# Two-layer hybrid attention and convolution backbone: key, query, value and statistics pieces moved in TensorE's order, and the rms root computed by ScalarE and VectorE

## The chip, the cores and the metric

One of the eight cores of a Trainium2 chip runs the whole program. The metric is the device time of one execution in microseconds (us). TensorE is called PE in the profile, its weight load PEld, VectorE DVE, ScalarE ACT, GpSimd POOL, and SyncE SP. SP issues nearly all DMAs, in order; each engine runs its own instructions in order and waits on semaphores for the others.

## What is computed

Two layers over 1024 latent tokens and 256 context tokens of width 1024. The second layer needs only keys and values of the context tokens. Cut to what matters:

```python
u   = h * (1 + scale) + shift                     # adaLN, per stream
p   = u @ w_in                                     # q k v z_a | s_b s_c s_h z_s | c_a c_g z_c | three gates
q   = rope(rms_norm(q) * q_gain);  k = rope(rms_norm(k) * k_gain)     # 8 query heads, 2 kv heads, 64 wide
o   = softmax(q k^T / 8) v                         # over context + latent keys, 128-query blocks
A   = (o * silu(z_a)) @ w_pa
B   = (s_b * conv3(s_c * s_h) * silu(z_s)) @ w_ps
hc  = conv31(c_a * sigmoid(c_g)) + b
C   = (silu(layer_norm(hc)) * silu(z_c)) @ w_pc + b_pc
h   = layer_norm(alpha * h + gate * ((sig(g_a) A + sig(g_b) B + sig(g_c) C) @ w_out))
# rms_norm(x) = x * rsqrt(mean(x^2) + 1e-6), per head
```

## The kernel before

Everything is held transposed: channels on the 128 partitions, tokens along the row, T = 1280 columns in layer 0 and 1024 in layer 1 (keys and values always 1280). A matrix product is made of fp32r parts, hi and lo: each `job(n)` makes one tile of 128 output channels as w_hi x_hi + w_lo x_hi + w_hi x_lo, over K = 8 blocks k of the contraction (K = 4 for the branch projections), in chunks of 512 columns. A k block so has 9 matmuls in layer 0 (6 of 512 and 3 of 256 columns) and 6 in layer 1. Jobs alternate between two PSUM slots (`SLOT`, n % 2); `sfree` says that a slot was read. The weights of job n come by an SP load (`load`, wraw, two buffers) and are split into wh and wl by GpSimd (`split`, a cast L584 and a subtraction L586 for each half); the load of job n waits for the split of job n-2, and the split waits for the end of job n-2.

A layer goes through these stages.

- **Query, key, value** (jobs 0 to 5: k, q0, q1, q2, q3, v). ScalarE copies each product to fc (`evac`), TensorE turns it into token order in pieces of up to four 128x128 transposes (`turn_piece`, L736), which go through two small PSUM banks in turns (`tbank(f)`, f % 2); `t_free` says that a piece was read. The pieces are put inside later jobs by hooks that run ahead of block k: K in job 1, Q0 in job 2, Q1 in job 3 (k = 2, 3, 5), the six pieces of the finished keys kd in job 4 (`keys_inside`, k = 1 to 6), Q2 and Q3 in job 5. For each of k, q0 to q3 ScalarE copies the pieces to raw (L1047) and squares (`square`), VectorE sums and scales (`mean_square`, L1348 and L1349), GpSimd raises to the power -1/2 (`rms`, L610, once in its queue for each n, behind the splits), and VectorE applies root, gain and rotation (`normed`, L1354 on). `k_hi` copies the turned keys to raw and rounds them to kT; `k_lo` on VectorE takes the remainder. raw has two buffers, and `s_rawfree` counts in the order K, Q0, Q1, KT0, KT1, Q2, Q3, V.
- **Attention** (`att_units`: 16 units of 10 key tiles for the latent queries in each layer, 4 short ones of 2 tiles in layer 0). In step kt of a unit TensorE turns four 128x128 blocks of the probabilities (`turn_probs`, L864) into bank kt % 2, ScalarE copies them (L1138), VectorE takes the remainder (L1454) and frees the bank. At even kt below 8 the scores of one head of the next unit are made (`scores`, L855), VectorE takes their maximum (L1428), and ScalarE the exponentials at the next odd kt (L1118). At kt = 5 the query of the unit after next is turned into bank 0 (`q_fill`, L841), copied by ScalarE (`q_hi`, L1110) and freed by VectorE (`q_lo`, L1420). `pv` (L877) multiplies two steps later. TensorE fills each step with matmuls of the 24 merge-gate jobs (`gate_slice`, L824), whose results ScalarE sends to DRAM.
- **Convolution** (jobs 30 to 61): z_a, conformer and short branch; the 31 taps run on VectorE (L1487).
- **z_c and the conformer norm** (jobs `I_ZC` to `I_ZC`+3). The channel sum and the sum of squares over partitions are matmuls with a matrix of ones (`stat`, L742), sent through the two small banks.
- **Merge** (24 jobs `I_M`+q of K = 4: branch B for q < 8, A for q < 16, C for the rest). SP loads the gate of each q (`load_gate`, waits for the use of gate q-2) and the attention branch (`load_ya`) between the weight loads; ScalarE takes the sigmoids and rounds the attention branch (`attn_hi`, L1230), VectorE multiplies (L1600, L1602), and in between does the conformer norm (L1555, L1574), `conf_out` and `attn_lo` (L1583).
- **Output** (8 jobs), the post norm, and between the layers the second modulation.

## Time and profile before

| | |
|---|---|
| median of three runs | 2879.9 us (2878.3 to 2881.8) |
| the profiled execution, its own time | 2872.59 us |
| its span in the profile | 2870.8 us |
| mean granted TensorE clock | 0.978 |
| busy: PE | 2677.8 us, 93% |
| busy: DVE | 1511.9 us, 53% |
| busy: ACT | 820.9 us, 29% |
| busy: POOL | 907.0 us, 32% |

The sum of busy TensorE time and its pauses is the span. Busy time contains matmuls at half clock, so a pause can cost more than its own length. Idle time of the other three engines costs nothing by itself. Durations in the rows are of one instruction or of a merged run ("x4"); a figure in square brackets is the engine's idle time before it and what ended that.

### The profile page before, as it was taken

What the parts mean: (1) busy time and instruction counts of PE and PEld (TensorE: products, weight loads), DVE (VectorE), ACT (ScalarE), POOL (GpSimd) and SP (SyncE); (2) the same over time, 40 slices, a digit from 0 to 9 for tenths busy, and PEclk for the clock granted to TensorE, in tenths of its full rate; (3) what the DMA queues carried; (4) which work ended last, traced back from release to release, by engine and by line L of the source; (5) the groups of instructions that cost most, each with busy time, mean ns of one, the idle gap of its engine ahead of it and who ended that gap; (6) DMA issues with size and microseconds to landing.
All of it is one profiled execution on the core that took longest, in us unless ns stands there. A gap on an engine that the chain in (4) does not pass through costs nothing.

```text
span 2870.8 us, 32327 instructions
## 1 busy us (share of the span) xinstructions
PE 2677.8 (93%) x13560; PEld 2197.1 (77%) x13560; DVE 1511.9 (53%) x1410; ACT 820.9 (29%) x1156; POOL 907.0 (32%) x819
## 2 busy tenths in 40 slices
PE   7999999999999999999995899999999999999993
PEld 4778888887887888788883677777788888877882
DVE  3454444441019988845626444554540199875635
ACT  3234444442100000142213434444441000014313
POOL 3431111111225333334531342111113355544550
PEclk8999999999999999999998999999999999999996
DMA  6010110011241111133343311101012211123421
GB/s 253 30 61 34 34 37 34 34 43 57 75 163 65 32 43 38 48 118 121 128 162 133 135 48 46 40 34 41 34 41 81 74 52 44 45 70 125 144 95 66
DMA packets 65521, 212.12 MB, mean 74 GB/s; under 512 B 7520, under 2 KB 10848, under 8 KB 63328
## 3 DMA queue, kind: packets, MB, share of 16 engines
q1 hardware_dynamic: 47520, 179.11, 17.8%
q10 hardware_dynamic: 17856, 30.94, 2.9%
q8 instruction: 108, 1.77, 0.3%
q14 instruction: 37, 0.30, 0.0%
HBM read 164.93 MB, written 45.09 MB: 73 GB/s over the span
## 4 chain that ended last, share of the span: by engine, by line
PE 83%; DVE 7%; ACT 6%; issue 2%; DMA 1%; POOL 1%; SPq 0%; ACTq 0%; DVEq 0%; POOLq 0%
PE PS L695 46%; PE PS L824 19%; PE PS L855 5%; PE PS L864 5%; PE PS L877 5%; DVE cv L1487 2%; ACT Pr L1118 2%; ACT PTh L1138 1%; PE PS L887 1%; DVE qTl L1420 1%; DVE e L1555 1%; PE PS L736 1%; PE PS L742 1%; DMA wmA<-wmod 1%; DVE e L1563 1%
## 5 line engine op out<-in xcount | busy, mean ns | idle before, releaser
L584 POOL CAST wh<-wraw 128x512 fp32r<-128x512 f32 (+1 forms) x376 | 297.7, 792 | 1476.5 <-PE PS L695 805.6
L586 POOL TENSOR_TENSOR wl<-wraw,wh 128x512 fp32r<-128x512 f32 (+1 forms) x376 | 534.3, 1421 | 30.1
L1454 DVE TENSOR_TENSOR PTl<-PS,PTh 128x512 fp32r<-128x512 f32 x328 | 226.9, 692 | 423.1 <-ACT PTh L1138 423.1
L1487 DVE SCALAR_TENSOR_TENSOR cv<-hc,vec,cv 128x1024 f32<-128x1024 f32 x360 | 441.7, 1254 | 8.2
L695 PE MATMUL PS<-Uh,wh 128*128 128x512 f32 (+1 forms) x1536 | 428.3, 377 | 17.0 <-ACT Uh L1023 15.7
L695 PE MATMUL PS<-Uh,wl 128*128 128x512 f32 (+1 forms) x1536 | 420.1, 371 | 0.0
L695 PE MATMUL PS<-Ul,wh 128*128 128x512 f32 (+1 forms) x1536 | 418.9, 371 | 0.0
L824 PE MATMUL PS<-Uh,wh 128*128 128x512 f32 (+1 forms) x960 | 358.4, 373 | 1.2 <-ACT stg L1076 1.2
L824 PE MATMUL PS<-Ul,wh 128*128 128x512 f32 (+1 forms) x960 | 359.3, 374 | 0.0
L824 PE MATMUL PS<-Uh,wl 128*128 128x512 f32 (+1 forms) x960 | 359.0, 374 | 0.0
L1138 ACT ACTIVATE PTh<-PS 128x512 fp32r<-128x512 f32 x328 | 196.4, 599 | 480.0 <-PE PS L864 479.0
L695 PEld LDWEIGHTS PS<-Uh,wh 128*128 128x128 f32 x1536 | 266.9, 190 | 70.8 <-issue 17.2
L695 PEld LDWEIGHTS PS<-Uh,wl 128*128 128x128 f32 x1536 | 268.1, 189 | 54.2
L695 PEld LDWEIGHTS PS<-Ul,wh 128*128 128x128 f32 x1536 | 266.6, 188 | 53.6
L864 PE MATMUL PS<-ident,Pr 128*128 128x128 f32 x1312 | 198.8, 274 | 37.6 <-DVE qTl L1420 37.0
L864 PEld LDWEIGHTS PS<-ident,Pr 128*128 128x128 f32 x1312 | 158.9, 141 | 83.1 <-DVE qTl L1420 45.5
L1428 DVE TENSOR_REDUCE nm<-PS 128x1 f32<-128x1280 f32 (+1 forms) x144 | 196.0, 1365 | 40.3 <-PE PS L855 40.1
L824 PEld LDWEIGHTS PS<-Uh,wh 128*128 128x128 f32 x960 | 180.9, 188 | 35.1 <-ACT stg L1076 1.7
L824 PEld LDWEIGHTS PS<-Uh,wl 128*128 128x128 f32 x960 | 180.9, 188 | 33.4
L824 PEld LDWEIGHTS PS<-Ul,wh 128*128 128x128 f32 x960 | 180.7, 188 | 33.2
L1118 ACT ACTIVATE Pr<-PS,nm 128x1280 f32<-128x1280 f32 (+1 forms) x144 | 177.4, 1232 | 29.3 <-DVE nm L1428 29.3
L855 PE MATMUL PS<-kT,qTh 128*128 128x512 f32 (+1 forms) x400 | 152.0, 380 | 12.4 <-ACT Pr L1118 9.4
(153 smaller groups left out, 3275.8 us busy)
## 6 DMA issues: line engine op xcount, KB each, us to landing
wraw<-w SPq DMA_DIRECT2D x140, 512.0 KB, 3.4
graw<-stg ACTq DMA_DIRECT2D x96, 256.0 KB, 2.0
e<-graw SPq DMA_DIRECT2D x24, 640.0 KB, 3.9
wraw<-w SPq DMA_DIRECT2D x48, 256.0 KB, 4.1
wmL<-wmod SPq DMA_DIRECT2D x8, 1536.0 KB, 11.7
e<-graw SPq DMA_DIRECT2D x24, 512.0 KB, 3.6
wmA<-wmod SPq DMA_DIRECT2D x8, 1024.0 KB, 12.9
hL<-hT_in SPq DMA_DIRECT2D x8, 640.0 KB, 21.8
```

Source lines behind the costliest of these rows:

```text
L584: nc.gpsimd.tensor_copy(wh[par][:, s], wraw[par][:, s]).then_inc(whi[par], 1)
L586: nc.gpsimd.tensor_tensor(wl[par][:, s], wraw[par][:, s], wh[par][:, s].bitcast(F32), ALU.subtract).then_inc(wsplit[par], 1)
L695: ins = mmul(PS[:, at + c:at + c + m], w[par][:, k * P:(k + 1) * P], x[:, k, c:c + m], start=(first and a == 0), stop=(last and a == 2))
L824: ins = mmul(PS[:, FB[x % 2]:FB[x % 2] + m], w[n % 2][:, k * P:(k + 1) * P], u[:, k, c:c + m], start=(r == 0), stop=(r == 23))
L855: ins = mmul(PS[:, s0 + c:s0 + c + m], x[un % 2][:, h * P:(h + 1) * P], kT[:, g, k0 * P + c:k0 * P + c + m], start=(a == 0), stop=(a == 1))
L864: ins = nc.tensor.transpose(PS[:, PT0[bank] + h * P:PT0[bank] + (h + 1) * P], Pr[:, un % 2, h, kt * P:(kt + 1) * P], ident[:])
L877: ins = mmul(PS[:, O0:O0 + 512], Vt[:, k0 + kt, g, :], x[b][:], start=(kt == 0 and a == 0), stop=(kt == nk - 1 and a == 1))
L1118: fn(Pr[:, g, h, :nk * P], PS[:, s0:s0 + nk * P], ACT.Exp, bias=nm[:, m:m + 1], accum_out=rs[:, g, h:h + 1]).then_inc(s_exp, 1)
L1138: fn(PTh[(sb + step) % 3][:], PS[:, PT0[bank]:PT0[bank] + 512], ACT.Copy).then_inc(pt_hi[bank], 1)
L1428: nc.vector.reduce_max(nm[:, m:m + 1], PS[:, s0:s0 + nk * P], AX_X, negate=True).then_inc(s_nm, 1)
L1454: tt(PTl[b][:], PS[:, PT0[bank]:PT0[bank] + 512], PTh[b][:].bitcast(F32), ALU.subtract).then_inc(pt_free[bank], 1)
L1487: ins = stt(cv[:, i, c0:c0 + n], hc[:, i, CPAD * who + c0 + tap:CPAD * who + c0 + tap + n], vec[:, l, wt:wt + 1], cv[:, i, c0:c0 + n], ALU ...
```

## The change

- **Queries, keys, values.** The piece order is K, Q0, KT0, KT1, Q1, Q2, Q3, V. The key pieces go into job 3, Q1's into job 4. ScalarE rounds keys and values straight from PSUM piece by piece (`k_hi`, `v_hi`), and VectorE takes the remainders from PSUM too and frees the bank (`k_lo`, `v_lo`); raw is used by the five normed operands alone. `t_free` becomes two semaphores, one for each bank.
- **The root.** `rms` leaves GpSimd. Behind each square ScalarE waits for the mean square and takes its square root; VectorE then has five small instructions: reciprocal r, h = r r, h = h ms, h = 1.5 - 0.5 h, r = r h.
- **Attention.** For units of 10 tiles `back` and `q_fill` come right behind `turn_probs` on TensorE, ahead of scores and pv, and `q_hi` ahead of that step's exponential on ScalarE. `q_fill(0)` moves ahead of the gate slice ("a", 2), whose `gate_out` moves behind `q_hi(0)`.
- **Conformer norm.** The mean statistic goes from ahead of job `I_ZC`+2 into job `I_ZC`+3 (k = 2, 3, 5), the variance statistic from ahead of job `I_M` into job `I_M`+2 (k = 1, 2, 3); `silu_z(2)` comes ahead of `mean`; `root` goes behind the sigmoid of q = 2; VectorE's reciprocal (L1555) and what follows from it move two to four jobs later; `load_ya` moves from q = 1, 1, 4, 5 to q = 3, 3, 5, 6. Jobs `I_M`+8 and `I_M`+16 wait for their operand block by block.

Changes of names and counters alone are left out of this diff, and so is the indentation they share.

```diff
@@ -55 +55 @@
-O_K, O_Q0, O_Q1, O_KT0, O_KT1, O_Q2, O_Q3, O_V = range(8)
+O_K, O_Q0, O_KT0, O_KT1, O_Q1, O_Q2, O_Q3, O_V = range(8)
@@ -528 +532 @@
             load_gate(1)
+        elif q > 1:
+            load_gate(q)
+        if q == 3:
...
             load_ya(1)
-        elif q > 1:
-            load_gate(q)
-        if q in (4, 5):
-            load_ya(q - 2)
+        if q in (5, 6):
+            load_ya(q - 3)
@@ -595 +600 @@
-    def rms(n):
-        pool.wait_ge(s_ms, l * 5 + n + 1)
-        nc.gpsimd.tensor_tensor(rstd[:, n % 2], ms[:, n % 2], mhalf[:], ALU.pow).then_inc(s_rstd, 1)
@@ -617 +617 @@
         table(0, 3, e[5], sinT[0])
-    rms(0)
...
     split(j0 + 5)
-    rms(1)
-    rms(2)
...
     split(j0 + 7)
-    rms(3)
-    rms(4)
@@ -802 +797 @@
     job(j0 + 2, T, Uh, Ul, tokens_inside(O_Q0, (2, 3, 5)))
-    job(j0 + 3, T, Uh, Ul, tokens_inside(O_Q1, (2, 3, 5)))
-    job(j0 + 4, T, Uh, Ul, keys_inside)
+    job(j0 + 3, T, Uh, Ul, keys_inside)
+    job(j0 + 4, T, Uh, Ul, tokens_inside(O_Q1, (2, 3, 5)))
@@ -888 +883 @@
+    def back_and_q(un, kt, nk):
+        if un > 0 and kt == back_at(nk):
+            back(un - 1)
+        if un + 2 < len(units) and kt == q_at(nk):
+            q_fill(un + 2)
...
         to_tokens(O_V, i)
+    q_fill(0)
...
     wait_slot(pe, j0 + 5)
-    q_fill(0)
@@ -909 +911 @@
         turn_probs(un, kt)
+        if nk > 2:
+            back_and_q(un, kt, nk)
...
             pv(step - 2)
+        gate_slice((un, kt))
         if nk == 2:
-            gate_slice((un, kt))
-        if un > 0 and kt == back_at(nk):
-            back(un - 1)
-        if un + 2 < len(units) and kt == q_at(nk):
-            q_fill(un + 2)
-        if nk > 2:
-            gate_slice((un, kt))
+            back_and_q(un, kt, nk)
@@ -953 +953 @@
     job(j0 + I_ZC + 1, T, Uh, Ul)
+    job(j0 + I_ZC + 2, T, Uh, Ul)
...
         pe.wait_ge(s_mod, 2)
-    pe.wait_ge(s_csum, 4 * l + 1)
-    stat(l, O_CMEAN, e[4])
-    job(j0 + I_ZC + 2, T, Uh, Ul)
-    job(j0 + I_ZC + 3, T, Uh, Ul)
-    pe.wait_ge(s_csum, 4 * l + 2)
-    stat(l, O_CVAR, e[5])
+    def mean_inside(k):
+        if k in (2, 3, 5):
+            pe.wait_ge(s_csum, 4 * l + 1)
+            stat(l, O_CMEAN, e[4], ((2, 3, 5).index(k),))
+    job(j0 + I_ZC + 3, T, Uh, Ul, mean_inside)
+    def var_inside(k):
+        if k >= 1:
+            pe.wait_ge(s_csum, 4 * l + 2)
+            stat(l, O_CVAR, e[5], (k - 1,))
     for q in range(N_G):
+        before = None
...
             pe.wait_ge(s_yb, KW * (l + 1))
+        if q == 2:
+            before = var_inside
         if q == 8:
-            pe.wait_ge(s_ya, KW * (l + 1))
+            before = lambda k: pe.wait_ge(s_ya, KW * l + k + 1)
         if q == 16:
-            pe.wait_ge(s_yc, KW * (l + 1))
-        job(j0 + I_M + q, T, *((YAh, YAl) if q // 8 == 1 else (Yh, Yl)))
+            before = lambda k: pe.wait_ge(s_yc, KW * l + k + 1)
+        job(j0 + I_M + q, T, *((YAh, YAl) if q // 8 == 1 else (Yh, Yl)), before)
@@ -1044 +1054 @@
-    def copy_raw(op):
-        if 8 * l + op >= 2:
-            act.wait_ge(s_rawfree, 8 * l + op - 1)
-        copy_pieces(op, raw[op % 2])
-        return raw[op % 2]
     def square(op):
-        Tn = op_width(l, op)
-        x = copy_raw(op)
-        if op != O_K:
-            act.wait_ge(s_ms, 5 * l + QKV_OPS.index(op))
-        fn(sq[:, :Tn], x[:, :Tn], ACT.Square).then_inc(s_sq, 1)
-    def k_hi(op, g):
-        x = copy_raw(op)
-        fn(kT[:, g, :], x[:], ACT.Copy).then_inc(s_khi, 1)
+        Tn, i = op_width(l, op), QKV_OPS.index(op)
+        if 5 * l + i >= 2:
+            act.wait_ge(s_rawfree, 5 * l + i - 1)
+        copy_pieces(op, raw[i % 2])
+        if i > 0:
+            act.wait_ge(s_ms, 5 * l + i)
+        fn(sq[:, :Tn], raw[i % 2][:, :Tn], ACT.Square).then_inc(s_sq, 1)
+        act.wait_ge(s_ms, 5 * l + i + 1)
+        fn(rstd[:, i % 2, :2 * Tn // P], ms[:, i % 2, :2 * Tn // P], ACT.Sqrt).then_inc(s_rstd, 1)
+    def k_hi(g):
+        for f, c, n in pieces(l, O_KT0 + g):
+            act.wait_ge(t_done, f + 1)
+            fn(kT[:, g, c:c + n], tbank(f, n), ACT.Copy).then_inc(s_khi, 1)
+    def v_hi():
+        for f, c, n in pieces(l, O_V):
+            act.wait_ge(t_done, f + 1)
+            fn(Vt[:, c // P:(c + n) // P, :, 0:HD],
+               tbank(f, n).rearrange("p (t g d) -> p t g d", g=NKV, d=HD), ACT.Copy).then_inc(s_vhi, 1)
@@ -1082 +1097 @@
     evac(2)
-    square(O_Q1)
-    evac(3)
...
         act.wait_ge(s_hst, 16 * KD)
-    k_hi(O_KT0, 0)
-    k_hi(O_KT1, 1)
+    k_hi(0)
+    k_hi(1)
+    evac(3)
+    square(O_Q1)
...
     gate_out(("a", 1))
-    x = copy_raw(O_V)
-    fn(Vt[:, :, :, 0:HD], x[:].rearrange("p (t g d) -> p t g d", g=NKV, d=HD),
-       ACT.Copy).then_inc(s_vhi, 1)
-    gate_out(("a", 2))
+    v_hi()
@@ -1123 +1135 @@
     q_hi(0)
+    gate_out(("a", 2))
@@ -1138 +1151 @@
             o_copy(un - 1)
+        if nk > 2 and un + 2 < len(units) and kt == q_at(nk):
+            q_hi(un + 2)
...
                 exps(un + 1, h)
-        if un + 2 < len(units) and kt == q_at(nk):
+        if nk == 2 and un + 2 < len(units) and kt == q_at(nk):
@@ -1210 +1225 @@
      silu_z(1)
+    silu_z(2)
...
     squares(12 * l, [cv[:, i, :T] for i in range(KW)])
-    silu_z(2)
     silu_z(3)
-    root(O_CVAR, KW)
@@ -1247 +1261 @@
         fn(e[2 + q % 2][:, :T], e[2 + q % 2][:, :T], ACT.Sigmoid).then_inc(s_sg, 1)
-        if q == 1:
+        if q == 2:
+            root(O_CVAR, KW)
+        if q == 3:
...
             attn_hi(1)
-        if q == 2:
+        if q == 4:
...
             conf_act(1)
-        if q == 3:
+        if q == 5:
@@ -1348 +1364 @@
-    def normed(op, n, Tn, A, B, dst):
+    def normed(n, Tn, A, B, dst):
...
         dve.wait_ge(s_rstd, 5 * l + n + 1)
+        r, h = rstd[:, n % 2, :H2], half[:, :H2]
+        st.done(nc.vector.reciprocal(r, r))
+        st.done(tt(h, r, r, ALU.mult))
+        st.done(tt(h, h, ms[:, n % 2, :H2], ALU.mult))
+        st.done(ts(h, h, -0.5, 1.5, ALU.mult, ALU.add))
+        st.done(tt(r, r, h, ALU.mult))
...
 @@ -1382 +1405 @@
-    def k_lo(op, g):
-        dve.wait_ge(s_khi, 2 * l + g + 1)
-        st.done(tt(kT[HD:P, g, :], raw[op % 2][HD:P, :], kT[HD:P, g, :].bitcast(F32), ALU.subtract))
-        dve.sem_inc(s_rawfree, 1)
+    def k_lo(g):
+        for i, (f, c, n) in enumerate(pieces(l, O_KT0 + g)):
+            dve.wait_ge(s_khi, 6 * l + 3 * g + i + 1)
+            tt(kT[HD:P, g, c:c + n], tbank(f, n)[HD:P], kT[HD:P, g, c:c + n].bitcast(F32),
+               ALU.subtract).then_inc(t_free[f % 2], 1)
+        wait_piece(dve, f)
...
+    def v_lo():
+        for i, (f, c, n) in enumerate(pieces(l, O_V)):
+            dve.wait_ge(s_vhi, 3 * l + i + 1)
+            tt(Vt[:, c // P:(c + n) // P, :, HD:P].rearrange("p t g d -> p (t g) d"),
+               tbank(f, n).rearrange("p (h d) -> p h d", d=HD),
+               Vt[:, c // P:(c + n) // P, :, 0:HD].rearrange("p t g d -> p (t g) d").bitcast(F32),
+               ALU.subtract).then_inc(t_free[f % 2], 1)
+        wait_piece(dve, f)
+        dve.sem_inc(s_kv, 1)
...
     mean_square(0, TALL)
-    normed(O_K, 0, TALL, e[0], e[1], k_out)
+    normed(0, TALL, e[0], e[1], k_out)
     mean_square(1, T)
+    k_lo(0)
+    k_lo(1)
...
         dve.wait_ge(s_hst, 16 * KD)
-    normed(O_Q0, 1, T, e[4], e[5], q_out(0))
+    normed(1, T, e[4], e[5], q_out(0))
     mean_square(2, T)
-    normed(O_Q1, 2, T, e[4], e[5], q_out(1))
-    k_lo(O_KT0, 0)
-    k_lo(O_KT1, 1)
+    normed(2, T, e[4], e[5], q_out(1))
...
     mean_square(4, T)
-    normed(O_Q2, 3, T, e[4], e[5], q_out(2))
-    normed(O_Q3, 4, T, e[4], e[5], q_out(3))
-    dve.wait_ge(s_vhi, l + 1)
-    st.done(tt(Vt[:, :, :, HD:P].rearrange("p t g d -> p (t g) d"),
-               raw[O_V % 2][:].rearrange("p (h d) -> p h d", d=HD),
-               Vt[:, :, :, 0:HD].rearrange("p t g d -> p (t g) d").bitcast(F32), ALU.subtract))
-    dve.sem_inc(s_rawfree, 1)
-    dve.sem_inc(s_kv, 1)
+    normed(3, T, e[4], e[5], q_out(2))
+    normed(4, T, e[4], e[5], q_out(3))
+    v_lo()
@@ -1551 +1581 @@
+    def inverse_std(k):
@@ -1608 +1640 @@
             tt(ACC[:, j, :T], ACC[:, j, :T], tmp, ALU.add).then_inc(s_mgf, 1)
-        if q == 0:
+        if q == 2:
+            inverse_std(2 * l)
+        if q == 3:
...
             conf_norm(1)
-        if q == 1:
+        if q == 4:
...
             conf_norm(3)
-        if 2 <= q < 4:
-            attn_lo(q - 2)
-        if 2 <= q < 6:
-            conf_out(q - 2)
+            attn_lo(0)
+            attn_lo(1)
+        if q == 5:
+            conf_out(0)
+            conf_out(1)
+        if q == 6:
+            conf_out(2)
+            conf_out(3)
@@ -1640 +1678 @@
     norm(2 * l + 1, lambda j: Z[:, j, :T], KD, 12 * l + KW)
+    inverse_std(2 * l + 1)
```

## Rows read from the trace of the kernel before

**Rows 1.** Page, busy time of TensorE and its weight load (share, instructions).

```profile
PE 2677.8 (93%) x13560; PEld 2197.1 (77%) x13560; DVE 1511.9 (53%) x1410; ACT 820.9 (29%) x1156; POOL 907.0 (32%) x819
```

**Rows 2.** Waits of TensorE, whole run: waiting <- releaser: us, times, longest.

```profile
PE PS L864 <- DVE qTl L1420: 37.0, 32, 1.6
...
PE PS L736 <- ACT raw L1047: 15.4, 6, 4.6
...
PE PS L695 <- DVE YAl L1583: 6.0, 2, 3.2
...
PE PS L742 <- ACT e L1212: 1.6, 1, 1.6
```

**Rows 3.** Timeline, layer 1 attention, kt = 5 and 6: start, us, what [idle before].

```profile
1859.07 0.60 PE L864 MATMUL PS<-ident,Pr 128*128 128x128 f32 x4
...
1859.97 0.60 PE L841 MATMUL PS<-ident,qd 128*128 128x128 f32 x4
...
1860.20 1.33 ACT L1118 ACTIVATE Pr<-PS,nm 128x1280 f32<-128x1280 f32 x1
...
1861.50 0.60 ACT L1110 ACTIVATE qTh<-PS 128x512 fp32r<-128x512 f32 x1
1862.13 0.69 DVE L1420 SCALAR_TENSOR_TENSOR qTl<-PS,qTh 128x512 fp32r<-128x512 f32 x1 [1.11 <-ACT qTh L1110]
...
1862.88 0.66 PE L864 MATMUL PS<-ident,Pr 128*128 128x128 f32 x4 [1.16 <-DVE qTl L1420]
```

**Rows 4.** Chain of work, two undisturbed runs of job matmuls, layer 0 and layer 1.

```profile
774.12 17.74 PE PS L695 x90
...
2566.28 22.32 PE PS L695 x96
```

**Rows 5.** Timeline, query and key stage, layer 0 and (from 1644) layer 1.

```profile
80.28 1.49 DVE L1354 TENSOR_TENSOR qn<-raw,rstd 128x1280 f32<-128x1280 f32 x1 [15.14 <-POOL rstd L610]
...
86.31 4.28 DVE L1374 TENSOR_TENSOR kd<-qa,qb 128x1280 f32<-128x1280 f32 x2
...
98.58 0.60 PE L736 MATMUL PS<-ident,kd 128*128 128x128 f32 x4
...
106.83 0.41 PE L736 MATMUL PS<-ident,kd 128*128 128x128 f32 x2 [3.73 <-ACT raw L1047]
...
125.15 0.60 PE L736 MATMUL PS<-ident,fc 128*128 128x128 f32 x4
...
166.13 0.47 PE L855 MATMUL PS<-kT,qTh 128*128 128x512 f32 x1 [1.50 <-DVE qTl L1420]
...
1644.65 0.60 PE L736 MATMUL PS<-ident,kd 128*128 128x128 f32 x4
...
1667.74 0.60 PE L736 MATMUL PS<-ident,fc 128*128 128x128 f32 x4
```

**Rows 6.** Busy time by stretch, from:to, us, engines, PEclk (granted clock), DMA share, GB/s.

```profile
107.00:111.00 4.00, 4.00 (x17) 3.49 (x17) 3.97 (x5) 1.84 (x3) 0.00 (x0) 0.65 0.00 0
...
1302.00:1306.00 4.00, 3.96 (x13) 3.28 (x14) 0.00 (x0) 1.72 (x2) 0.57 (x1) 0.61 0.52 203
...
2638.00:2642.00 4.00, 3.24 (x14) 2.66 (x15) 0.70 (x1) 1.20 (x2) 1.29 (x1) 1.00 0.60 197
```

**Rows 7.** Timeline, conformer norm and merge, layer 0.

```profile
1206.88 4.08 PE L742 MATMUL PS<-e,ones 128*128 128x512 f32 x6 [3.34 <-issue]
...
1240.10 1.28 ACT L1212 ACT_TABLE_LOAD   x1
...
1243.42 8.15 DVE L1555 RECIPROCAL e<-e 128x1280 f32<-128x1280 f32 x1 [21.09 <-ACTq L1215]
...
1267.38 0.43 SPq L467 DMA_DIRECT2D wraw<-w  x1
...
1273.80 0.44 POOL L584 CAST wh<-wraw 128x256 fp32r<-128x256 f32 x1 [6.21 <-DMA wraw<-w]
```

**Rows 8.** Page, DMA issues: what, queue, count, KB each, median us to landing.

```profile
wraw<-w SPq DMA_DIRECT2D x48, 256.0 KB, 4.1
```

More of the change, by code:

```diff
@@ L344, in build @@
         ms = small("ms", [P, 2, 2 * NTOK])
+        half = small("half", [P, 2 * NTOK])
         rstd = small("rstd", [P, 2, 2 * NTOK])
-        mhalf = small("mhalf", [P, 2 * NTOK])
         nm = small("nm", [P, 8])
@@ L385, in build @@
         t_done = sem("piece_done")
-        t_free = sem("piece_read")
+        t_free = [sem(f"piece_read{i}") for i in range(2)]
         s_rawfree = sem("raw_free")
@@ L400, in build @@
         s_ms = sem("mean_square")
-        s_rstd = sem("rstd")
+        s_rstd = sem("rms_root")
         s_kd = sem("k_duplicated")
@@ L449, in wait_job, with wait_piece @@
             eng.wait_ge(mm[n % 2], jobs_of(n))
+        def wait_piece(eng, f):
+            eng.wait_ge(t_free[f % 2], f // 2 + 1)
         def wait_slot(eng, n):
@@ L729, in piece_wait @@
                 if f >= 2:
[L730 removed]
+                    wait_piece(pe, f - 2)
             def turn_piece(l, op, i, srcs):
@@ L737, in turn_piece, with stat @@
                 ins.then_inc(t_done, 1)
-            def stat(l, op, src):
-                for f, c, n in pieces(l, op):
+            def stat(l, op, src, which=(0, 1, 2)):
+                for f, c, n in [p for i, p in enumerate(pieces(l, op)) if i in which]:
                     piece_wait(f)
@@ L902, in _ @@
                     if h == 3:
-                        pe.wait_ge(t_free, last_piece(l, O_V) + 1)
+                        for f, _, _ in pieces(l, O_V):
+                            wait_piece(pe, f)
                         q_fill(1)
@@ L947, in _ @@
                     if l == 0 and i == I_CONF + 4:
-                        pe.wait_ge(t_free, last_piece(l, O_OT + 3) + 1)
+                        for f, _, _ in pieces(l, O_OT + 3):
+                            wait_piece(pe, f)
                         for k in range(KD):
```

22 lines of the change are left out of this document (10 added, 12 removed).

## The prediction

> **What bounds the kernel now.** First the busy times: TensorE is busy 2677.8 us of a span of 2870.8 us, 93% [rows 1], so a gain has to be a pause of TensorE, or a stretch at half clock behind one. Second, its waits [rows 2]: the pauses that this change can reach are those at the turned probabilities (L864, 37.0 us in 32 pauses), at the turned pieces (L736, 15.4 us in 6), at the attention branch of the merge (L695 behind L1583, 6.0 us in 2) and at the variance statistic (1.6 us). Longer single pauses, at the post norm and between the layers, lie where nothing is moved. Third, timelines around one pause of each kind [rows 3, 5, 7], to see which engine ended late and what it did just before. Fourth, the granted clock behind pauses [rows 6]: after a pause of 3.7 us it is 0.65 over four microseconds, after one of 3.2 us 0.61 (a mix of the levels 2.4 and 1.2 GHz), after one of 2.8 us 1.00. A pause above some 3 us so costs about 1.6 us more (4 us at 0.61 do the work of 2.4). Undisturbed, 90 job matmuls of layer 0 take about 17.5 us, so a block k of 9 takes 1.745 us; in layer 1, 96 take 22.3, so a block of 6 takes 1.395 [rows 4].
>
> **Attention.** In step 5 of a unit TensorE turns the probabilities at 1859.07, runs pv, turns the query at 1859.97, then fills; ScalarE's exponential (1860.20, 1.33 us) stands ahead of the query copy (1861.50), so VectorE's remainder ends at 1862.82 and the next turn starts at 1862.88 after a pause of 1.16 [rows 3]. After the change the query is turned about 0.4 behind 1859.07 and ready 0.6 later, at 1860.1; its copy takes the exponential's place at 1860.2 and ends at 1860.8; VectorE, which has the probabilities' remainder till 1861.0, needs 0.69 and is done at 1861.7. TensorE's own work in the step ended at 1861.72. The pause goes. What is late next: the exponential moves 0.5 back and ends, with its sum, near 1862.2, and the scores of head 3, on TensorE at 1862.1, wait some 0.15 for it. Net 1.05 us a unit. It holds for the 16 long units of layer 0 and the 14 of layer 1 that have a unit two further: 30 x 1.05 = **31.5 us saved**. Bounds: 1.18 each if the exponential doesn't matter (35.4), 0.9 if the first fill is short (27). The short units keep their order. `back` at step 3 is moved too, but the step has no pause in the waits; 0.
>
> **Keys, queries, values.** The key pieces pause because raw is held by Q1: ScalarE's copy waits for VectorE's product, which waited for GpSimd's power. From the first key piece in job 4 (98.58) to the first Q2 piece in job 5 (125.15) pass 26.57 us [rows 5]. Own work is 8 blocks of 1.745 and six groups of four transposes of about 0.4 (from the distance 1859.07 to 1859.97, less pv's two matmuls [rows 3]): 16.4. The excess, 10.2 us, is the pauses 3.73 and 3.16 and the clock behind them. Layer 1: 1644.65 to 1667.74 is 23.09; 7 x 1.395 + 1.745 + 2.4 = 13.9; excess 9.2. After the change keys and values use no raw, and a piece is free after ScalarE's 0.60 and VectorE's 0.69 for 128x512 [rows 3], 2 us after its turn; the same bank is wanted two blocks, 3.5 to 4.2 us, later. **19.4 us saved**, if the keys are there a job earlier. They are wanted near 98.6 - 15.0 = 83.6. VectorE had the mean square at 80.28 - 15.14 = 65.1 [rows 5]; a table load of 1.28 [rows 7] and a short root bring 66.7; five small instructions cost between 0 and 5 x 0.69 (the nearest row, 128x512), I take 1.2 since 20 columns are little; from there on it took 80.28 to 90.6, 10.3 us. Ready at 78.2, 5.4 us early; for layer 1 I estimate 4. That is where the root counts: with the power, which VectorE awaited for 15.14 us, they would come at 90.6, 7 us late. GpSimd loses ten powers, nothing waits for that. VectorE now stands in `k_lo` through job 3 and the queries' `normed` comes behind: Q0 to Q3 then end some 20 us ahead of the scores. ScalarE's new wait for the mean square holds back the next pieces by one reduction, 1.5 us, beside a bank distance of 3.5.
>
> The switch to the root's table is weighed once more. The Trainium skill (ScalarE: Activation LUTs, Rules for kernel authors) says to group functions by table set and to budget about 2.7 us for a switch; the trace's load takes 1.28 [rows 7]. By its price, an estimate from that page, the keys of layer 1 would be ready 2.6 instead of 4 us early: the sum stays, rival C becomes a little likelier.
>
> Values: the third piece now waits for VectorE's 0.69 as well: +0.7 in each layer. The first scores paused 1.50 for the query's remainder [rows 5]; `q_fill(0)` and `q_hi(0)` now come a gate slice earlier, so that goes, I take it for both layers: -3.0 + 1.4 = **1.6 us saved**.
>
> **Conformer norm and merge, what is saved.** Layer 0: the pause of 3.22 before branch A goes, since block 3 asks for its operand 5 us later than block 0 did, and the clock stays up (1.6) [rows 2, 6]; the variance pause of 1.6 goes. Against it: the first pause (3.34 before the mean statistic [rows 7]) now ends only when `silu_z(0)`, which waits for the same sum, has freed its slot, about 1.3 longer (ScalarE, 1280 columns [rows 3]); its clock fall stays. -6.4 + 1.3 = -5.1. Layer 1: -2.8 for branch A, +1.0 for silu, +1.6 because its first pause, which I estimate under 3 us as its sums have 1024 columns, then comes over it and the clock falls: -0.2. Together 5.3 us saved. The statistics' own matmuls cost the same inside a job.
>
> **And what is lost.** SP's queue is the place. `load_ya(2)` at q = 5 waits for `attn_lo(0)`, and the weights of job M+6 stand behind it. `attn_lo(0)` used to be early; now VectorE has, from the end of job M+2: product 1.5, reciprocal 8.15 [rows 7], then product, two norms, product, two norms and itself, 7 x 1.49 (the length of a two-input operation on 1280 columns [rows 5]) = 20.1 us. M+6 is due three jobs after M+2, 3 x 4 x 1.745 = 21.0 us. The weight load needs 0.4 to be issued behind the other, 6.4 us to land when it follows an attention load (1267.38 to 1273.80, where GpSimd waited for it [rows 7]; the median of such loads is 4.1 [rows 8]), and GpSimd's first half a cast of 0.44 and a subtraction of about twice that. 20.1 + 0.4 + 6.4 + 1.3 = 28.2: TensorE stands still for 7.2 us. Layer 1, with VectorE's terms at 0.8: 16.0 + 8.1 against 16.7, 7.4; I take 7.0, the transfer being no larger than that of layer 0 while its neighbour is smaller. With two clock falls of 1.7: **17.7 us lost** (9.6 with 4.1 us to land and no clock fall; 20 if GpSimd is slowed). Merge stage: 12.4 us lost in all.
>
> **Sum.** -31.5 - 19.4 - 1.6 + 12.4 = -40.1 us. From the profiled execution's own 2872.6 that is 2832.5; it lies 7.3 under the median of the runs shown, so on the median 2879.9 the forecast is **2839.8**, with 2828 to 2852 by the bounds above.
>
> **Rivals.** A: as summed. B: job M+6 doesn't stall, because VectorE comes to `attn_lo(0)` some 8 us sooner than I count; against it stands the reciprocal of 8.15, which nothing shortens: 2839.8 - 17.7 = 2822. C: the keys come late after all, or ScalarE's and VectorE's mutual waits hold a piece: for it speaks that three engines now hand over in a ring, against it the 5 us of room; half of the 19.4 lost, 2850. D: the pause in attention is exchanged for one at the scores of head 3, as the exponential is now 0.5 late; half the gain, 2856. E, the other side: the exponentials behind `q_hi` run late far enough that every unit pays. Without any attention gain 8.6 us remain saved; slower by over 0.2% (5.8 us) begins where each of the 30 units loses 0.48 us against before, that is where head 3's scores wait 1.7 us instead of 0.15. At 0.6 a unit it gives 2889. Against it: the copy that goes ahead takes only 0.60 us [rows 3]. That the change doesn't take effect is hardly possible: the orders are written out by hand, one queue an engine.
>
> **How the numbers follow.** A 58%, B 12%, C 10%, D 14%, E 3%, and 3% for gain and loss meeting near no change. 2824 to 2856 leaves out most of B, E, and the last: some 2 in 10. Faster by over 0.2% (about what a measurement of this kernel can tell from no change) has 0.94, within 0.03, slower 0.03.
>
> **What the profile after would show.** L864 out of TensorE's waits down to a few us; no pause at the key pieces and the clock at 1.00 there; a pause of about 1.6 at the third value piece and none at the first scores; a pause of 4.6 before job `I_ZC`+2; none at branch A; a new wait of about 7 us on GpSimd's split in each layer before job M+6, SP standing at `load_ya`. The forecast is wrong if that last wait is missing, or if L855 takes over from L864.

## The result and the profile after

The changed kernel takes 2837.3 us (median of four runs, 2834.9 to 2844.2) where the kernel before, run beside it, takes 2879.1: a ratio of 0.986, 95% interval 0.984 to 0.988, or some 41 us less. The forecast was 2839.8, from 2824 to 2856. The profiled execution of the changed kernel has an own time of 2837.68 us and a span of 2835.9; against the profiled one of before it is 34.9 us shorter.

Busy times and waits of TensorE after the change (page; then waiting <- releaser: us, times, longest), beside [rows 1, 2]:

```profile
PE 2681.1 (95%) x13560; PEld 2206.2 (78%) x13560; DVE 1538.1 (54%) x1472; ACT 819.8 (29%) x1163; POOL 876.2 (31%) x808
```

```profile
PE PS L690 <- POOL wl L591: 12.3, 2, 6.5
PE PS L850 <- ACT Pr L1130: 9.3, 22, 1.0
PE PS L690 <- ACT hc L1211: 8.4, 2, 4.6
PE PS L731 <- DVE Vt L1419: 6.7, 2, 5.0
PE PS L859 <- DVE qTl L1450: 5.4, 8, 1.5
```

TensorE's work is nearly as long as it was (2677.8), its pauses have shrunk. L864 is now L859: 37.0 us of waits for the query's remainder have become 5.4: 1.5 in each of two short units and 0.4 in six long ones. The turned pieces (L736, now L731) wait 6.7 us instead of 15.4, and for values, no longer for raw. Branch A's 6.0 us are gone. New are 12.3 us before two merge jobs, behind GpSimd's split. Before job `I_ZC`+2, behind `silu_z(0)`, stand 8.4, where the mean statistic had paused 3.3 and 2.7. The waits of the scores for the exponentials, 9.3 us in 22, are those of before (9.4 in 22).

Step 5 and 6 of an attention unit of layer 1 after the change, beside [rows 3]:

```profile
1828.65 0.60 PE L859 MATMUL PS<-ident,Pr 128*128 128x128 f32 x4
1829.08 0.60 PE L836 MATMUL PS<-ident,qd 128*128 128x128 f32 x4
1829.78 0.59 ACT L1122 ACTIVATE qTh<-PS 128x512 fp32r<-128x512 f32 x1
1830.25 1.33 ACT L1130 ACTIVATE Pr<-PS,nm 128x1280 f32<-128x1280 f32 x1
1830.52 0.68 DVE L1450 SCALAR_TENSOR_TENSOR qTl<-PS,qTh 128x512 fp32r<-128x512 f32 x1
1831.26 0.66 PE L859 MATMUL PS<-ident,Pr 128*128 128x128 f32 x4
```

From one turn of the probabilities to the next pass 2.61 us where 3.81 passed, with no pause ahead of the second.

The end of the query stage, layer 0 (timeline):

```profile
128.20 1.49 DVE L1364 TENSOR_REDUCE ss<-sq 128x20 f32<-128x1280 f32 x1 [4.37 <-ACT sq L1067]
129.80 0.27 DVE L1371 RECIPROCAL rstd<-rstd 128x20 f32<-128x20 f32 x1
...
140.04 0.27 DVE L1371 RECIPROCAL rstd<-rstd 128x20 f32<-128x20 f32 x1
...
149.05 1.29 DVE L1419 TENSOR_TENSOR Vt<-PS,Vt 128x512 fp32r<-128x512 f32 x2
...
149.88 0.66 PE L731 MATMUL PS<-ident,fc 128*128 128x128 f32 x2 [5.04 <-DVE Vt L1419]
```

VectorE stands 4.37 us for the square of Q3, though Q2's square has long been reduced; `normed` of Q2 starts at 129.80, that of Q3 at 140.04 and ends at 149.0. The value remainder, which frees the bank, is queued behind both. The forecast had 1.6 us here.

The merge of layer 0 (timeline), what leads to the pause before job M+6:

```profile
1244.81 8.15 DVE L1587 RECIPROCAL e<-e 128x1280 f32<-128x1280 f32 x1
...
1261.88 2.89 DVE L1615 TENSOR_TENSOR YAl<-e,YAh 128x1280 fp32r<-128x1280 f32 x2
...
1263.39 0.32 SPq L528 DMA_DIRECT2D e<-yAd  x1
1263.76 0.43 SPq L471 DMA_DIRECT2D wraw<-w  x1
...
1268.19 1.35 POOL L589 CAST wh<-wraw 128x256 fp32r<-128x256 f32 x1 [15.60 <-DMA wraw<-w]
1269.62 0.72 POOL L591 TENSOR_TENSOR wl<-wraw,wh 128x256 fp32r<-128x256 f32 x1
...
1270.48 1.41 PE L690 MATMUL PS<-Yh,wh 128*128 128x512 f32 x3 [6.47 <-POOL wl L591]
```

The chain is the one of the forecast: SP can issue the attention load only when the first remainder has ended at about 1263.3, and the weights stand behind it. Busy time by stretch behind the pauses before M+6 and before `I_ZC`+2, layer 0 (columns as in [rows 6]), shows the clock at its lower level of 1.2 GHz for four microseconds, and at a key piece it stays at 2.4:

```profile
1270.48:1274.48 4.00, 4.00 (x11) 3.32 (x12) 0.00 (x0) 2.68 (x3) 2.93 (x6) 0.50 0.81 308
1187.12:1191.12 4.00, 4.00 (x11) 3.32 (x12) 0.00 (x0) 1.07 (x1) 1.58 (x2) 0.50 0.31 96
84.00:88.00 4.00, 4.00 (x26) 3.53 (x25) 1.11 (x2) 1.53 (x3) 2.68 (x3) 1.00 0.08 11
```

Lengths of the stages on TensorE, in us, layer 0 / layer 1. Each is the distance between two starts in the traces: first K piece, first key piece, first gate slice, first scores; for attention, the first turn of the probabilities and the last gate matmul behind it; first job of branch A.

| kernel | K to keys | keys to gate | gate to scores | attention | end of attention to branch A |
|---|---|---|---|---|---|
| before | 43.4 / 35.0 | 41.0 / 37.0 | 26.6 / 29.4 | 583.3 / 482.2 | 528.7 / 418.0 |
| after | 28.4 / 23.0 | 45.6 / 39.5 | 31.7 / 28.5 | 567.0 / 467.6 | 534.3 / 424.6 |
| root alone | 43.5 / 35.0 | 30.6 / 27.7 | 26.6 / 29.4 | 583.2 / 481.9 | 527.8 / 417.5 |
| attention alone | 43.4 / 35.0 | 40.8 / 38.6 | 26.6 / 29.4 | 565.4 / 467.9 | 534.1 / 419.5 |
| moves, with the power | 35.4 / 25.1 | 48.1 / 39.8 | 35.1 / 33.0 | 566.9 / 467.7 | 538.0 / 425.1 |
| root and attention | 43.4 / 35.0 | 30.6 / 27.7 | 26.6 / 29.4 | 565.5 / 467.7 | 532.9 / 417.5 |

### The profile page after: what moved, and what is told of

The parts are those of the page before. It is cut to its first block, busy times and chain, and to the rows that moved or that the text cites. A ratio compares the mean times of both kernels' runs of the same rounds, so it can differ in the third digit from the quotient of the medians.

```text
span 2835.9 us, 32387 instructions
## 1 busy us (share of the span) xinstructions
PE 2681.1 (95%) x13560; PEld 2206.2 (78%) x13560; DVE 1538.1 (54%) x1472; ACT 819.8 (29%) x1163; POOL 876.2 (31%) x808
## 3 DMA queue, kind: packets, MB, share of 16 engines
q1 hardware_dynamic: 47520, 179.11, 17.9%
q8 instruction: 108, 1.77, 0.3%
## 4 chain that ended last, share of the span: by engine, by line
PE 84%; DVE 9%; ACT 4%; issue 1%; DMA 1%; SPq 0%; POOL 0%; ACTq 0%; DVEq 0%
PE PS L690 46%; PE PS L819 20%; PE PS L850 6%; PE PS L872 5%; PE PS L859 5%; DVE cv L1517 3%; PE PS L882 1%; DVE e L1587 1%; ACT Pr L1130 1%; PE PS L731 1%; PE PS L737 1%; DMA wmA<-wmod 1%; DVE e L1595 1%; ACT PTh L1151 1%; PE PS L836 0%
## 5 line engine op out<-in xcount | busy, mean ns | idle before, releaser
L690 PE MATMUL PS<-Uh,wh 128*128 128x512 f32 (+1 forms) x1536 | 429.3, 377 | 25.1 <-ACT Uh L1033 15.3
L819 PEld LDWEIGHTS PS<-Uh,wl 128*128 128x128 f32 x960 | 181.5, 189 | 35.1
L859 PE MATMUL PS<-ident,Pr 128*128 128x128 f32 x1312 | 198.1, 273 | 6.1 <-DVE qTl L1450 5.4
L859 PEld LDWEIGHTS PS<-ident,Pr 128*128 128x128 f32 x1312 | 159.8, 140 | 48.1 <-DVE qTl L1450 9.6
## 6 DMA issues: line engine op xcount, KB each, us to landing
wmA<-wmod SPq DMA_DIRECT2D x8, 1024.0 KB, 12.4
hL<-hT_in SPq DMA_DIRECT2D x8, 640.0 KB, 21.5
```

Source lines behind the costliest of these rows:

```text
L690: ins = mmul(PS[:, at + c:at + c + m], w[par][:, k * P:(k + 1) * P], x[:, k, c:c + m], start=(first and a == 0), stop=(last and a == 2))
L819: ins = mmul(PS[:, FB[x % 2]:FB[x % 2] + m], w[n % 2][:, k * P:(k + 1) * P], u[:, k, c:c + m], start=(r == 0), stop=(r == 23))
L859: ins = nc.tensor.transpose(PS[:, PT0[bank] + h * P:PT0[bank] + (h + 1) * P], Pr[:, un % 2, h, kt * P:(kt + 1) * P], ident[:])
```

## The experiments

All times are medians with the ratio to the kernel before, run beside them (it took 2875.7 us beside e1 to e4 and 2879.1 to 2880.4 beside the others). What a kernel saves against the changed one is the difference of ratios times 2880 us. The intervals are about 0.002 to each side (6 us, and some 8 for the difference of two), so for small edits the pauses in the trace decide. The span of one trace doesn't: executions of the same code differ by several microseconds, as the last section shows.

| kernel | median us | ratio, 95% interval |
|---|---|---|
| changed kernel | 2837.3 | 0.9858 (0.9839 to 0.9877) |
| e1, remainders early | 2821.5 | 0.9803 (0.9779 to 0.9827) |
| e5, attention load late | 2820.8 | 0.9801 (0.9778 to 0.9823) |
| e2, Q2 normed first | 2833.3 | 0.9845 (0.9826 to 0.9863) |
| e3, root alone | 2852.6 | 0.9914 (0.9890 to 0.9937) |
| e4, attention alone | 2851.3 | 0.9905 (0.9885 to 0.9925) |
| e6, moves with the power | 2859.0 | 0.9938 (0.9915 to 0.9960) |
| e9, root and attention | 2828.9 | 0.9826 (0.9806 to 0.9846) |
| e7, e1 and e2 | 2819.2 | 0.9791 (0.9772 to 0.9811) |
| e10, e7 and e5 | 2814.2 | 0.9782 (0.9768 to 0.9796) |
| e11, e10 with the mean moved back | 2814.4 | 0.9772 (0.9757 to 0.9787) |

**The pause before job M+6: e1 and e5.** The first makes VectorE earlier, the second changes only SP's order.

```diff
@@ e1, VectorE, q == 3 and 4 @@
     if q == 3:
+        attn_lo(0)
+        attn_lo(1)
         conf_norm(0)
...
         conf_norm(3)
-        attn_lo(0)
-        attn_lo(1)
@@ e5, SP @@
-    if q in (5, 6):
-        load_ya(q - 3)
+    if q in (6, 7):
+        load_ya(q - 4)
```

> The changed kernel with VectorE's two remainders of the attention branch, attn_lo(0) and attn_lo(1), made at the head of q = 3, ahead of the four conformer norms, instead of behind them. Theory (SP's queue is what starves job M+6: load_ya(2) waits for attn_lo(0), and the weights of M+6 stand behind it): the remainders end some 10 us earlier, load_ya(2) no longer holds SP, GpSimd has the weights of M+6 in time, the pauses of 6.47 and 5.81 us before job M+6 and the clock falls behind them go: 12.3 + 3.4 = 15.7 us at most, I expect 13 to 16 us less than the changed kernel, about 2823 us. The conformer activations start 3 us later, nothing waits for them. Rival (the weights are late because the attention loads share the DMA engines with them, or GpSimd is slowed by VectorE): both pauses stay at 5 us or more, and the time is that of the changed kernel, 2837.

> The changed kernel with nothing but SP's order changed: load_ya(2) and load_ya(3) at q = 6 and 7 instead of 5 and 6, so that the weights of job M+6 and M+7 are issued ahead of the transfer that waits for attn_lo(0); VectorE does exactly what it did. Theory (SP's queue is the cause): the pause before M+6 falls from 6.47 and 5.81 us to under 1 us in each layer, about 13 to 15 us less than the changed kernel, 2823 us; a pause of a few us can move to job M+8, whose weights now stand behind load_ya(2). Rival (VectorE's lateness itself, through the products of the merge or GpSimd's splits, is what holds the job): the pauses stay above 4 us, since VectorE's order is the same.

Both are about 16 us faster than the changed kernel by the ratios, within some 8. The two pauses and the clock behind them were worth at most 12.3 + 3.4 = 15.7. In e5 TensorE waits for GpSimd's split in the whole run only this much:

```profile
PE PS L690 <- POOL wl L591: 2.0, 2, 1.2
```

Its VectorE is no earlier; the rows of layer 0 in e5 show the weights of M+6 issued at 1260.34, ahead of the attention load, while the remainder still starts at 1268.09:

```profile
1250.22 8.15 DVE L1587 RECIPROCAL e<-e 128x1280 f32<-128x1280 f32 x1
1260.34 0.43 SPq L471 DMA_DIRECT2D wraw<-w  x1
1264.47 0.40 POOL L589 CAST wh<-wraw 128x256 fp32r<-128x256 f32 x1 [6.47 <-DMA wraw<-w]
1268.09 3.63 DVE L1615 TENSOR_TENSOR YAl<-e,YAh 128x1280 fp32r<-128x1280 f32 x2
1269.80 0.32 SPq L528 DMA_DIRECT2D e<-yAd  x1
```

So the place in SP's queue is the cause, and not VectorE's lateness by itself. Nor does a pause of a few microseconds appear at M+8: what is left are 0.8 and 1.2 us before M+7. In e1 layer 1 keeps 2.1 us. There the attention load is issued at 2563.07, the weights right behind it at 2563.44, and GpSimd has them 5.4 us later. Whether the two transfers slow each other, or SP's short wait alone does it, neither run separates; e10 below takes that order away, and the pause with it.

**The third value piece: e2.**

```diff
@@ VectorE, query stage @@
     mean_square(3, T)
-    mean_square(4, T)
     normed(3, T, e[4], e[5], q_out(2))
+    mean_square(4, T)
     normed(4, T, e[4], e[5], q_out(3))
```

> The changed kernel with VectorE's order at the end of the query stage changed: mean_square(3), normed(3), mean_square(4), normed(4) instead of both means first. Theory (the third value piece of layer 0 pauses 5.03 us because VectorE stands for the square of Q3 before it has touched Q2, so that everything behind it, the value remainder included, is late): normed(3) starts some 4 us earlier, the pause falls from 5.03 to the 1.6 us of the bank's own chain, and the clock stays up: 4 to 5 us less than the changed kernel in layer 0, nothing in layer 1, where the pause is 1.63 already; about 2833 us. Rival (VectorE's work of the stage is simply too much, because its operations are stretched while GpSimd splits weights): the pause stays above 4 us.

The pause goes from 5.04 to the size of the forecast, and layer 1 stays as it was:

```profile
145.85 0.41 PE L731 MATMUL PS<-ident,fc 128*128 128x128 f32 x2 [1.42 <-DVE Vt L1419]
1672.27 0.41 PE L731 MATMUL PS<-ident,fc 128*128 128x128 f32 x2 [1.63 <-DVE Vt L1419]
```

From the first gate slice to the first scores pass 25.5 us instead of 31.7, 6.2 less: 3.6 of pause, and the granted clock in the four microseconds behind it, which was 0.50 and is 1.00. The medians differ by 4 us and the ratios by 0.0013, within their intervals; the trace carries this one.

**Root or moves: e3 and e6.** e3 is the kernel before with the new root; e6 the changed kernel with the old one.

```diff
@@ e3, against the kernel before @@
-    nc.gpsimd.tensor_tensor(rstd[:, n % 2], ms[:, n % 2], mhalf[:], ALU.pow).then_inc(s_rstd, 1)
...
+    fn(rstd[:, i % 2, :2 * Tn // P], ms[:, i % 2, :2 * Tn // P], ACT.Sqrt).then_inc(s_rstd, 1)
...
+    st.done(nc.vector.reciprocal(r, r))
+    st.done(tt(h, r, r, ALU.mult))
+    st.done(tt(h, h, ms[:, n % 2, :H2], ALU.mult))
+    st.done(ts(h, h, -0.5, 1.5, ALU.mult, ALU.add))
+    st.done(tt(r, r, h, ALU.mult))
```

> The kernel before with the root alone: GpSimd's power is replaced by ScalarE's square root behind each square and VectorE's five small instructions; all piece orders, raw's use and the merge stay as before. Theory of the forecast (root and moved keys are both needed; the root only brings the finished keys 12 us earlier): raw is then freed 10 us or more earlier as well, so that the key pieces' pauses (3.73 and 3.16 us in layer 0, like ones in layer 1) go without any move: 15 to 19 us less than before, about 2862 us. Rival (the pauses come from raw being shared by keys and queries, whatever makes the root): the key pieces still pause 3 us or more in each layer, and less than 5 us are saved. The first value and query pieces may also move by a microsecond.

> The changed kernel with GpSimd's power in the places where it stood before instead of ScalarE's root and VectorE's five instructions; all moves stay. The root alone, on the kernel before, took the key pauses away without any move, 10.3 us in layer 0 and 9.4 in layer 1, as much as root and moves together. Theory now (what held the key pieces was the 15 us wait for the power, the moves are not needed): with the power and the moves the finished keys come at about 90 us while job 3 wants them at 84, so that each layer waits 6 to 8 us at the first key piece, and the queries end later still: some 15 to 20 us more than the changed kernel, about 2855 us. Rival (the moves do half of the work themselves, by taking the keys out of raw): less than 5 us more than the changed kernel.

With the root alone the key pieces, still turned in job 4 out of raw, run through in layer 0 without a pause, where [rows 5] has 3.73 before the third and another behind it:

```profile
98.78 0.60 PE L727 MATMUL PS<-ident,kd 128*128 128x128 f32 x4
100.99 0.60 PE L727 MATMUL PS<-ident,kd 128*128 128x128 f32 x4
103.17 0.38 PE L727 MATMUL PS<-ident,kd 128*128 128x128 f32 x2
```

From the first K piece to the first gate slice e3 takes 74.1 / 62.7 us and the changed kernel 74.0 / 62.5, against 84.4 / 72.0 before. The whole gain of the stage is the root's. By the medians e3 is 23 us under the kernel before, by the ratio 25, by the profiled spans 20.

What the edit shortened was for the most part a queue. The mean square was there at 65.14, and GpSimd, before it came to the power, did the split of a job, which itself waited for TensorE till 67.05, and two tables. Rows of the kernel before:

```profile
67.05 0.61 POOL L584 CAST wh<-wraw 128x512 fp32r<-128x512 f32 x1 [5.39 <-PE PS L695]
...
73.78 2.97 POOL L592 TENSOR_TENSOR e<-sinT,gain 128x1280 f32<-128x1280 f32 x1
76.68 3.57 POOL L610 TENSOR_TENSOR rstd<-ms,mhalf 128x20 f32<-128x20 f32 x1
```

Of the wait of 15.14 us the power is 3.57 (in layer 1 3.53 of 8.30). An obvious rival to the new root, the old power put ahead of the splits in GpSimd's queue, was not run. From these rows I estimate that the keys' product would then have started near 65.1 + 3.6 = 68.7 instead of 80.28, against 66.74 with the new root. So the runs show what an earlier root is worth, not that it had to leave GpSimd.

The other half of the square: with the moves and the power, VectorE waits for GpSimd as long as ever and TensorE for the keys.

```profile
79.58 1.49 DVE L1378 TENSOR_TENSOR qn<-raw,rstd 128x1280 f32<-128x1280 f32 x1 [15.18 <-POOL rstd L615]
85.59 4.25 DVE L1398 TENSOR_TENSOR kd<-qa,qb 128x1280 f32<-128x1280 f32 x2
89.89 1.12 PE L741 MATMUL PS<-ident,kd 128*128 128x128 f32 x4 [6.89 <-DVE kd L1398]
...
161.63 0.66 PE L741 MATMUL PS<-ident,fc 128*128 128x128 f32 x2 [8.60 <-DVE Vt L1420]
```

e6 is 22 us slower than the changed kernel (23 by the ratios). Layer 0 pauses as expected; layer 1 pauses 1.98 at the keys, not 6 to 8, and 3.83 at the values. The moves need the earlier root; the root doesn't need the moves.

**Attention: e4.**

```diff
@@ TensorE, kernel before @@
         turn_probs(un, kt)
+        if nk > 2:
+            back_and_q(un, kt, nk)
...
             pv(step - 2)
+        gate_slice((un, kt))
         if nk == 2:
-            gate_slice((un, kt))
-        if un > 0 and kt == back_at(nk):
-            back(un - 1)
-        if un + 2 < len(units) and kt == q_at(nk):
-            q_fill(un + 2)
-        if nk > 2:
-            gate_slice((un, kt))
+            back_and_q(un, kt, nk)
@@ ScalarE @@
+        if nk > 2 and un + 2 < len(units) and kt == q_at(nk):
+            q_hi(un + 2)
         if un + 1 < len(units):
```

> The kernel before with the attention change alone: for units of 10 tiles back and q_fill right behind turn_probs on TensorE, and q_hi ahead of the exponential of that step on ScalarE. Theory (the pause of 1.16 us at step 6 of each of 30 units is the query copy behind the exponential): 1.0 to 1.1 us less in each unit, 30 to 33 us less than before, about 2848 us; the 37.0 us of TensorE's waits for the query's remainder fall to some 5. Rival (the pause is exchanged for one at the scores of head 3, since the exponential is 0.5 us later): half of it, 16 us less than before, with a new wait of about 0.5 us a unit at the scores.

The ratio says 27 us, the medians 24, the profiled spans 21.5. The stage lengths give 17.9 us for the 16 units of layer 0 and 14.3 for the 14 of layer 1, 32.2 in all, 1.07 a unit. Waits of TensorE in e4:

```profile
PE PS L855 <- ACT Pr L1121: 9.3, 22, 1.0
PE PS L864 <- DVE qTl L1425: 5.4, 8, 1.5
```

The scores wait for the exponentials as before, so the pause wasn't exchanged for another. What is missing in the spans lies in stages that e4 leaves alone, most of it in one: from the end of attention to branch A it took 534.1 us against 528.7 in layer 0 (the last section shows why).

**Root and attention, nothing moved: e9.** The edits of e3 and e4 together.

> The kernel before with the root and the attention order alone: no piece is moved, keys and values still go through raw, and conformer norm and merge stay as before. Theory (these two parts bring all that the change brings, and the moved keys and statistics only cost): the separate savings, about 23 and 25 us by their runs, add to 48: 2828 us by the medians; by the stages of the traces (10.3 + 9.4 in the query stage, 17.9 + 14.3 in attention) 52, 2824 us. Either way 9 to 13 us less than the changed kernel. Rival (the moved keys and values are worth something once attention is faster, or both parts spend the same slack): 2837 us or more, no better than the whole change.

It is 9 us faster than the changed kernel by the ratios (0.9826 against 0.9858, the intervals overlap) and 8 by the medians; its profiled span is 12.4 shorter. By the stages the two parts add: the query stage is e3's to 0.1 us and attention e4's to 0.2. What the changed kernel has beyond e9, the moved pieces and the restructured merge, so costs more than it brings as it stands. It does so by the pauses that it brought: e10 below keeps all the moves without the long pauses before M+6 and at the value piece, and is 13 us faster than e9 by the ratios, with intervals apart. Of that, 7.3 us lie between the end of attention and branch A in layer 0.

**Fixes together: e7, e10, e11.** e7 has the edits of e1 and e2, e10 that of e5 as well. e11 puts the mean statistic back:

```diff
+    pe.wait_ge(s_csum, 4 * l + 1)
+    stat(l, O_CMEAN, e[4])
     job(j0 + I_ZC + 2, T, Uh, Ul)
-    job(j0 + I_ZC + 3, T, Uh, Ul, mean_inside)
+    job(j0 + I_ZC + 3, T, Uh, Ul)
@@ ScalarE @@
-    silu_z(2)
     mean(O_CMEAN, KW)
     squares(12 * l, [cv[:, i, :T] for i in range(KW)])
+    silu_z(2)
```

> The changed kernel with both edits that shortened it: the attention remainders at the head of q = 3 and normed(3) ahead of mean_square(4). Theory (the two pauses, 12.3 us before M+6 and 3.4 at the value piece, are independent): the savings add, 14 to 16 and 4, about 18 to 20 us less than the changed kernel, 2818 us. Rival (what is late is VectorE as a whole, and the second edit's gain is given back in the merge): no better than the first edit alone, 2822.

> The changed kernel with the two shortening edits (remainders at the head of q = 3, normed(3) ahead of mean_square(4)) and load_ya(2) and load_ya(3) at q = 6 and 7. Theory (in layer 1 the load of the attention branch still ran just ahead of the weights of job M+6, which is the 1.8 to 2.1 us that were left before that job): this pause goes too, 2 us less than with the two edits alone, 2817 us. Rival (the weights' landing time behind any other load sets it, or the pause moves on to job M+8): no change from 2819. A gain of 2 us is near what the comparison can tell, so the pause in the trace decides.

> The same with the mean statistic put back ahead of job I_ZC+2, as in the kernel before, and silu_z(2) back behind the squares; the variance statistic stays inside job M+2. Theory (moving the mean statistic only made the first pause longer, 4.1 to 4.6 and 3.8 us against 3.3 and 2.8, because the next job now waits for silu_z(0) behind the same sum): the pauses return to 3.3 and 2.8, and in layer 1 the clock then stays up; about 1.2 us less in layer 0 and 2.6 in layer 1, 3 to 4 us less than its neighbour, about 2813 us. Rival (the copies of the statistic in the open cost as much as the pause saves, or the variance statistic comes too late for job M+2): no change, or a few us more. The pauses and the clock in the trace decide.

e7 saves 19 us by the ratios, near the sum of its parts (16 and 4). In e10 the wait of 1.77 us before M+6 in layer 1 is gone, and 0.78 appears before M+7; the time can't be told from e7's. In e11 both pauses return to their old length. By the stages e11 gains 0.7 us in layer 0 and 1.8 in layer 1, and the ratio can't be told from e10's. Where the rest of the expected 3 to 4 us is, the stretch behind its pause in layer 1 shows; the second row is the same place in e9, behind a pause of the same 2.75 us:

```profile
2506.43:2510.43 4.00, 4.00 (x7) 2.01 (x8) 0.00 (x0) 3.01 (x4) 2.84 (x3) 0.57 0.03 8
```

```profile
2515.08:2519.08 4.00, 4.00 (x14) 2.65 (x15) 1.02 (x1) 2.90 (x4) 2.87 (x3) 1.00 0.03 8
```

The clock fell in one and stayed up in the other. e10 and e11, at 0.978 and 0.977, are the fastest kernels here, some 22 to 25 us under the changed one.

## Why the prediction was right, and where it wasn't

- **Attention, -31.5.** Measured 16.2 + 14.6 = 30.8, in e4 32.2. Mechanism and size hold, the rows of step 5 as well: the copy at 1829.78 in the place of the exponential, the remainder's end at 1831.2. Rival D is out by the scores' unchanged 9.3 us.
- **Keys and queries, -19.4.** Measured 10.4 + 9.5 = 19.9 by the stages up to the gate slices. The size is right, since it was read off the pauses themselves, whatever ends them; the cause is wrong. The step that failed is "After the change keys and values use no raw": it gave the gain to the moves, and the root only the part of making them possible. But the term's own first sentence names the cause, the product that waited for the power. With the new root the keys' product starts 13.5 us earlier in layer 0 (66.74 in e3 against 80.28) and 6.5 in layer 1, and Q0's, which frees raw for the first key operand, 19 us earlier (85.31 against 104.57). That is more than the pauses of 2.2 to 4.6 us that it had to cover, and e3 shows that it is enough alone. In the own work of the term "six groups of four transposes" is misread as well: the third piece of each key operand is a pair ("x2").
- **Keys ready at 78.2, wanted at 83.6.** Ready at 80.1, wanted at 84.14; in layer 1 2.5 us early (1614.57 against 1617.07) for an estimated 4. The table load that the chain counts with 1.28 cost nothing: it ran at 63.99, under VectorE's reduction, and in layer 1 there is none at this place. The five small instructions took 0.28 and four times 0.18, with gaps 1.17 us in e3, against an assumed 1.2. So the first product started at 67.15, where the forecast comes to 67.9. From there the keys took 13.0 us instead of 10.3, most of it in the two subtractions of kd, 6.64 instead of 4.28. The seven microseconds that the power would cost came out as 6.89 in layer 0 of e6 and as 1.98 in layer 1, where VectorE had awaited the power 8.30 us and not 15.14. Rival C did not come about.
- **Third value piece, +0.7.** True in layer 1 (1.63). In layer 0 it was 5.04, 3.4 more, with a clock fall behind it. The step that failed is "Q0 to Q3 then end some 20 us ahead of the scores": they ended 12.5 us ahead (149.0 against 161.49), and `v_lo`, queued behind them on VectorE, frees a bank that TensorE wanted at 144.8. The question "what is queued behind the waiting instruction" was asked for ScalarE and not for VectorE's wait for the last square.
- **First scores, -3.0.** The pause went in both layers (1.50 and 1.46). In layer 1 gate to scores is 0.95 shorter, with 0.7 of the value piece in it.
- **Conformer norm and merge, saved.** The pause before `I_ZC`+2 is 4.56 in layer 0, as forecast, and 3.81 in layer 1; the pauses at branch A and the variance are gone. The idea that a pause under 3 us keeps the clock is refuted (below): the +1.6 for layer 1 stood on one row, and in other executions the same pause did bring the clock down.
- **Job M+6, +17.7.** Pauses of 6.47 and 5.81 for 7.2 and 7.0. VectorE's chain from the end of M+2 (1264.01, the end of M+5, less 21.0, is 1243.0) to the first remainder is 20.3 us for 20.1. GpSimd had the weights 4.4 us after their issue, for 6.4; the median of the page [rows 8] was nearer. Both loads were issued 0.4 us behind an attention load, and a third such, in e1, took 5.4, so why the forecast's row was long isn't shown. From GpSimd's first cast to the start of the job passed 2.3 us for 1.3 (the cast alone 1.35 for 0.44). The cause, SP's queue, is shown by e1 and e5.
- **The sum.** Forecast -40.1; -34.9 between the two profiled executions, -41 by the ratio. The merge lost 10.9 us for 12.4 (5.2 in layer 0, 5.7 in layer 1, by the shift of the first row behind the output jobs against that of the first row ahead of the stage; different paces of TensorE are in it). The 5.2 us that are missing in the profiled pair are 5.8 between gate and scores (the two layers give +5.2 - 0.9 = +4.2 where -1.6 was forecast), 0.7 in attention, 0.6 before the first K piece, less 1.5 in the merge and 0.5 at the keys. That the median came to 2.5 us of the forecast is partly luck: the value piece cost more than forecast and the merge less, and the kernel before was profiled in one of its shorter executions, the changed one in a median one.

## What to carry to other kernels

When an operand becomes ready much earlier, first ask whether that alone frees the buffer that another edit is meant to go round; here an earlier root did all that a new piece order was credited with, and of the 15.14 us that VectorE waited for the old one, 3.57 were its own work. So look too at what stands ahead of the late instruction in its queue. A load that waits for an engine belongs behind the weights of the next jobs in a shared queue: moving two loads by one job was worth 16 us. And of an engine that is made to wait for something new, follow its queue to the last instruction that frees a bank.
